# Modulation for the first norm in two column groups, x in four pieces at the head of the queue, and the sample keys one slot later

## The chip, the cores and the metric

The kernel runs on one core of one Trainium2 chip. The metric is the device time of one execution in microseconds (us), the median of several runs. TensorE (PE) multiplies, VectorE (DVE) and ScalarE (ACT) work on elements, GpSimd (POOL) and SyncE (SP) mostly issue DMAs. Each engine runs its own list of instructions in order and waits on semaphores.

## What is computed

One decoder layer, in float32, for a prompt of 512 tokens and for a sample group of 8 sequences with 4 tokens each, which attend over 4096 cached tokens.

```python
sh1, sc1, g1, sh2, sc2, g2 = split(silu(c) @ w_mod + b_mod, 6)
h = rmsnorm(x, norm1_w) * (1 + sc1) + sh1
rq, rk, rv, rg, mq, mk, mv = split(h @ w_in)
...  # retention on rq, rk, rv, rg; block-sparse attention (MoBA) on mq, mk, mv
x = x + g1 * (concat([ret_out, moba_out]) @ w_out)
h2 = rmsnorm(x, norm2_w) * (1 + sc2) + sh2
x = x + g2 * ((silu(h2 @ w_gate) * (h2 @ w_up)) @ w_down)
```

## The kernel before

**Slots.** The engines share a numbering of slots, one tile of 128 weight columns against the 512 prompt tokens in each. Slots 0 to 27 (`NT` = 28) hold the input projection, 13 to 28 also the prompt's attention, 30 to 42 retention (four pairs of heads, three slots each), 43 to 50 the output projection, 51 to 53 the second norm, 54 to 97 the gate and up tiles, 98 to 121 the down tiles. A tile is 24 matmuls of 512 columns: the high part of the weights with the high and the low part of the activations, and the low part of the weights with the high part of the activations. ScalarE makes the high halves (`split_hi`, L561; `split_out`, L566), VectorE the low ones (`split_in_place`, L1603; `split_out`, L1596).

**Keys and values of the sample group.** Beside the tiles each slot s takes group s of the gathered cache (64 groups, eight per sequence): POOL gathers K (L478), VectorE transposes it (`turn_keys`, L1634), TensorE multiplies it with the queries (`keys`, L1027), and 12 slots later (`LAG`) `weigh` (L1082) multiplies the probabilities with V. After the eighth group of a sequence the engines work through its tail, one step in each of the next slots, by t = s mod 8: at 0 the block sums (L1640) and `block_gates` (L1053), at 1 the selection (L1652), at 2 `row_max` (L1674), at 3 the bias (L1680), the exponentials on ScalarE (L590) and the first turn of the probabilities, at 4 `fold_heads` of the sequence before (L1695), at 5 the denominators, at 6 their inverse and the block diagonal of a coming sequence (L1623), at 7 `keep_out`. In every slot `slot_head` comes before the tile and `slot_rest` behind it.

**Modulation.** `w_mod` is read in 24 chunks of 256 columns, 1 MB each. Eight of them make shift and scale of the first norm before any slot: two buffers (`raw`) alternate, so each load from the third on waits for TensorE (L404 to L407). TensorE multiplies a chunk in four groups of 32 rows (`rows_by_k`, L957), VectorE adds the groups up (`keep_mod`, `fold_groups`, four instructions), TensorE turns a pair of chunks (`turn_mod`), VectorE adds the bias (`modulation`). After the eighth come the gains, then the transposed x is scaled and shifted by ScalarE (L627), column group k by column group. The other 16 chunks come in the slots of `MOD_AT`, each loaded into `rawm` when the one before is done (`mod_in`, L578).

**The head's order.** x is one DMA of 2 MB behind the first two chunks. ScalarE squares xs and the four row blocks of x, VectorE inverts, ScalarE takes the root and scales all of x (L552). TensorE transposes x after all eight chunks, and takes `keys(0)` ahead of the first tile.

**The second norm.** In slot 51 VectorE makes the inverse of the mean square, ScalarE the root after its `slot(52)` (L849 to L851), and VectorE waits for it behind its own `slot_head(52)` (L1962, L1963) before it scales x.

Of the kernel before, what the change touches and what calls it, by code (L numbers as in the profile page):

```python
# [9 lines left out]
P = 128  # L10
# [26 lines left out]
NMOD = 6 * DM // CHUNK  # L37
NMA = 2 * DM // CHUNK
# [17 lines left out]
LAG = 12  # L56
# [12 lines left out]
S_END = NG + LAG  # L69
# [7 lines left out]
def constants():  # L77
# [18 lines left out]
    put("pad0", np.zeros((P, 6)))  # L96
    put("ones", np.ones((P, P)))
# [8 lines left out]
    put("sum_pv", (p % 32)[:, None] == ht[None, :])  # L106
# [41 lines left out]
def decoder_step(nc, x_prompt, x_sample, cache_k, cache_v, state_ret, page_table, c_prompt, c_sample,  # L148
# [74 lines left out]


# [34 lines left out]
    unit = lambda n: ffa[:, n] if n < 10 else ffb[:, n - 10]  # L259
# [35 lines left out]
    s_mev, s_mtp, s_mp = sem("mod_copied+2"), sem("mod_turned+1"), sem("mod_pair_kept+1")  # L295
# [4 lines left out]
    s_xx = sem("x_turned")  # L300
    s_xst, s_hs = sem("xs_turned"), sem("asT_ready")
# [12 lines left out]
    s_srot, s_sqt, s_sqe, s_sa = sem("s_rotated"), sem("s_qk_turned"), sem("s_qkT"), sem("s_scores")  # L314
    s_sad, s_so, s_soc, s_sot = sem("s_decayed"), sem("s_out"), sem("s_out_copied"), sem("s_out_turned")
    s_ssq, s_srs, s_srn, s_srt = sem("s_squares"), sem("s_rstd"), sem("s_normed"), sem("s_norm_turned")
    s_sas, s_ssg = sem("s_ret_mixed"), sem("s_gate_silu")
# [32 lines left out]
    B_IN = NMA // 2  # L350

# [9 lines left out]
    mod_at = lambda n: slice((NMA + n) * CHUNK, (NMA + n + 1) * CHUNK)  # L361
# [22 lines left out]
    def _(sp):  # L384
# [16 lines left out]
        sp.dma_start(xP[:, :, :], x_prompt[0].rearrange("(i p) d -> p i d", p=P)).then_inc(s_x, 16)  # L401
        sp.dma_start(xs[:, :], x_sample.rearrange("b t d -> (b t) d")).then_inc(s_xs, 16)
        sp.dma_start(pt[:, :], page_table.rearrange("b n -> (b n)").partition_broadcast(P)).then_inc(s_pt, 16)
        with sp.Fori(1, NMA // 2) as i:  # L404
            for u in range(2):
                sp.wait_ge(s_md, 2 * i + u - 1)
                chunk(u, w_mod_v, bass.ds((2 * i + u) * CHUNK, CHUNK))  # L407
        for u in range(2):
            sp.wait_ge(s_md, NMA - 1 + u)
            chunk(u, w_in_v, slice(COL_OF[u], COL_OF[u] + CHUNK))  # L410
        sp.dma_start(ct[:, P + 8:], const[:, P + 8:NA]).then_inc(s_const, 16)
        sp.dma_start(rawm[:, :, :], w_mod_v[:, :, mod_at(0)]).then_inc(s_wm, 16)
# [26 lines left out]
        sp.wait_ge(s_sas, 1)  # L439
# [35 lines left out]
    def _(pool):  # L475
# [27 lines left out]
        for g in range(2, NG):  # L503
            pool.wait_ge(s_kt, g - 1)
            gather(g)
            if g == R_PAIR + 4:
# [3 lines left out]
            if g == R_OUT + 3:  # L510
# [5 lines left out]
            if g == R_OUT + 4:  # L516
# [3 lines left out]
            if g == R_OUT + 5:  # L520
                masked_k(0)
                masked_k(1)
            if g == R_SAMPLE + 5:
                pool.wait_ge(s_so, 1)
                pool.tensor_tensor(state[:, :, :, :], state[:, :, :, :],
                                   C("c_dec_s").unsqueeze(1).unsqueeze(3).broadcast_to((P, NB_SEQ, HP, HD)), ALU.mult).then_inc(s_sdc, 1)
            if R_SAMPLE + 6 <= g < R_SAMPLE + 9:
                b = 2 * (g - R_SAMPLE - 5)
# [4 lines left out]
    def _(act):  # L533
# [5 lines left out]
        act.wait_ge(s_x, 16)  # L539
        act.drain()  # L540
        for i in range(TT):
            last = act.activation(sq[:, :], xP[:, i, :], ACT.Square, accum_out=st[:, i:i + 1])
            if i < TT - 1:
                act.drain()
# [4 lines left out]
        act.drain()  # L549
# [28 lines left out]
        def mod_in(n):  # L578
            act.wait_ge(s_md, NMA + n)
            act.dma_start(rawm[:, :, :], w_mod_v[:, :, mod_at(n)]).then_inc(s_wm, 16)  # L580
# [364 lines left out]
    def _(pe):  # L945
# [1264 lines left out]
```

## Time and profile before

| | |
|---|---|
| median of 3 runs | 1119.65 us (1116.27 to 1120.73) |
| profiled execution | 1118.47 us |
| its span, first to last instruction | 1116.6 us |
| mean granted TensorE clock | 0.927 |
| TensorE matmuls busy | 979.4 us (88%) |
| VectorE busy | 656.7 us (59%) |
| ScalarE busy | 339.4 us (30%) |
| HBM read | 260.04 MB |

The profile is of one execution, 1118.47 us long, of which the span of the instructions is 1116.6. Busy times are sums over the whole span. Where a row ends in brackets, the engine was idle that long before it, and the name behind the arrow is what ended the idle time. A granted clock of 1.00 is 2.4 GHz, 0.50 is 1.2 GHz.

### The profile page before, as it was taken

To read this page: it belongs to the slowest core of one execution; us is meant where nothing else is said; L and a number is where in the kernel's file an instruction comes from. 1 tells how busy PE (TensorE), PEld (TensorE's weight loads), DVE (VectorE), ACT (ScalarE), POOL (GpSimd) and SP (SyncE) were. 2 spreads that over 40 slices of the span, in tenths; PEclk is the share of its full clock that TensorE was granted. 3 is DMA by queue.
4 is the path that set the end of the run, shared out by engine and by line. 5 is a ranking of instruction groups with operands and counts; after the bars stand their busy time and mean duration, and the time that the engine had idled before them with its cause. 6 is when DMAs were issued, how large, how long until landed. Compare 5 with 4: busy or idle time off the path is not lost.

```text
span 1116.6 us, 20916 instructions
## 1 busy us (share of the span) xinstructions
PE 979.4 (88%) x7847; PEld 684.4 (61%) x7847; DVE 656.7 (59%) x1152; ACT 339.4 (30%) x678; POOL 91.0 (8%) x90
## 2 busy tenths in 40 slices
PE   3669999999999657467987699999999999999996
PEld 1356766766776334244753476767677777777775
DVE  3555775676676487776656657543266555553344
ACT  4331233324224324224214414333234222221113
POOL 0011110000010021101400123000000000000000
PEclk8679999999999788787988689999999999999998
DMA  9846878877777768576888567977847798887662
GB/s 294 303 150 232 309 252 280 294 263 265 272 261 261 229 229 307 189 257 208 267 300 281 188 212 249 276 226 227 272 123 216 193 233 236 226 242 237 202 227 80
DMA packets 220355, 267.01 MB, mean 239 GB/s; under 512 B 12785, under 2 KB 175929, under 8 KB 212066
## 3 DMA queue, kind: packets, MB, share of 16 engines
q1 hardware_dynamic: 111586, 123.21, 35.1%
q10 hardware_dynamic: 99456, 75.38, 22.0%
q0 software_dynamic: 9216, 67.11, 16.8%
q8 instruction: 62, 1.02, 0.4%
q14 instruction: 35, 0.29, 0.1%
HBM read 260.04 MB, written 5.64 MB: 238 GB/s over the span
## 4 chain that ended last, share of the span: by engine, by line
PE 73%; DVE 13%; DMA 5%; DVEq 3%; ACT 3%; issue 2%; SPq 1%; ACTq 0%
PE banks L1001 13%; PE banks L1002 12%; PE banks L1003 12%; PE banks L961 6%; PE banks L1016 4%; PE banks L1036 4%; PE banks L1091 4%; DVE KT L1638 4%; PE banks L1017 4%; PE banks L1018 4%; DMA raw<-in_w_mod 2%; PE banks L1179 2%; DVEq L1539 2%; DMA raw<-in_w_out 1%; PE banks L1164 1%
## 5 line engine op out<-in xcount | busy, mean ns | idle before, releaser
L1001 PE MATMUL banks<-ahi,whi 128*128 128x512 f32 x416 | 170.9, 411 | 0.0
L571 ACT ACTIVATE whi<-raw 128x1024 fp32r<-128x1024 f32 (+1 forms) x76 | 78.7, 1035 | 301.3 <-PE banks L1003 157.5
L1638 DVE STREAM_TRANSPOSE KT<-K 128x2048 f32<-128x2048 f32 x64 | 147.7, 2308 | 37.0 <-PE banks L1036 29.7
L1002 PE MATMUL banks<-alo,whi 128*128 128x512 f32 x416 | 164.2, 395 | 0.0
L1003 PE MATMUL banks<-ahi,rawlo 128*128 128x512 f32 x416 | 164.0, 394 | 0.0
L1601 DVE TENSOR_TENSOR rawlo<-raw,whi 128x1024 fp32r<-128x1024 f32 (+1 forms) x76 | 91.4, 1203 | 61.9 <-ACT whi L571 59.1
L478 POOL DMA_INDIRECT K<-in_cache_k,kidx x64 | 64.7, 1011 | 581.8 <-DVE KT L1638 538.2
L1001 PEld LDWEIGHTS banks<-ahi,whi 128*128 128x128 f32 x416 | 79.6, 191 | 31.5 <-issue 13.6
L1036 PE MATMUL banks<-KT,qbd 128*32 128x128 f32 x2048 | 75.2, 291 | 25.5 <-DVE KT L1638 24.2
L1016 PE MATMUL banks<-ahi,whi 128*128 128x512 f32 x224 | 93.6, 418 | 1.2 <-DVE rawlo L1608 0.9
L1003 PEld LDWEIGHTS banks<-ahi,rawlo 128*128 128x128 f32 x416 | 79.3, 191 | 17.7
L1002 PEld LDWEIGHTS banks<-alo,whi 128*128 128x128 f32 x416 | 79.9, 192 | 15.1
L1017 PE MATMUL banks<-alo,whi 128*128 128x512 f32 x224 | 88.7, 396 | 0.0
L1018 PE MATMUL banks<-ahi,rawlo 128*128 128x512 f32 x224 | 88.6, 396 | 0.0
L1036 PEld LDWEIGHTS banks<-KT,qbd 128*32 128x32 f32 x2048 | 57.7, 116 | 42.5 <-DVE KT L1638 20.9
L1091 PE MATMUL banks<-V,pT 128*32 128x512 f32 x368 | 54.0, 650 | 3.4 <-issue 2.0
L1016 PEld LDWEIGHTS banks<-ahi,whi 128*128 128x128 f32 x224 | 42.6, 190 | 18.3 <-issue 7.6
L1608 DVE TENSOR_TENSOR rawlo<-raw,whi 128x1024 fp32r<-128x1024 f32 x28 | 34.2, 1223 | 30.4 <-ACT whi L564 14.8
L655 ACT ACTIVATE pm<-banks,st 128x128 f32<-128x128 f32 (+3 forms) x32 | 16.6, 522 | 112.4 <-DVE st L1763 112.4
L1018 PEld LDWEIGHTS banks<-ahi,rawlo 128*128 128x128 f32 x224 | 42.8, 191 | 9.7
L1017 PEld LDWEIGHTS banks<-alo,whi 128*128 128x128 f32 x224 | 42.7, 191 | 7.7
L1551 DVE TENSOR_TENSOR xtmp<-xtmp,banks 32x256 f32<-32x256 f32 x90 | 37.5, 417 | 7.0 <-issue 0.4
(304 smaller groups left out, 1447.6 us busy)
## 6 DMA issues: line engine op xcount, KB each, us to landing
V<-in_cache_v SPq DMA_DIRECT2D x184, 256.0 KB
rawm<-in_w_mod ACTq DMA_DIRECT2D x15, 1024.0 KB
zT<-in_cache_v SPq DMA_DIRECT2D x52, 256.0 KB
raw<-in_w_in ACTq DMA_DIRECT2D x12, 1024.0 KB
raw<-in_w_gate ACTq DMA_DIRECT2D x22, 512.0 KB
raw<-in_w_up ACTq DMA_DIRECT2D x22, 512.0 KB
srw<-in_w_gate SPq DMA_DIRECT2D x22, 512.0 KB, 5.4
srw<-in_w_up SPq DMA_DIRECT2D x22, 512.0 KB, 6.7
```

Source lines behind the costliest of these rows:

```text
L571: act.activation(whi[t % 2][:, 0:kd, :], raw[u][:, 0:kd, t % 2 * P:(t % 2 + 1) * P], ACT.Copy).then_inc(s_hi, 1)
L961: last = pe.matmul(out[32 * g:32 * g + 32, 0:CHUNK], lhs(k), rhs[:, k, :], start=(first and k < 4), stop=(final and k >= kd - 4))
L1001: pe.matmul(out[:, :], whi[t % 2][:, k, :], hi(k), start=(first and n == 0), stop=False)
L1002: pe.matmul(out[:, :], whi[t % 2][:, k, :], lo(k), start=False, stop=False)
L1003: last = pe.matmul(out[:, :], low[:, k, :], hi(k), start=False, stop=(final and n == kd - 1))
L1016: pe.matmul(DB[:, :], whi[m % 2][:, k, :], ahi[:, k, :], start=(k == 0), stop=False)
L1017: pe.matmul(DB[:, :], whi[m % 2][:, k, :], alo[:, k, :], start=False, stop=False)
L1018: last = pe.matmul(DB[:, :], wlow[:, k, :], ahi[:, k, :], start=False, stop=(k == KT - 1))
L1036: last = pe.matmul(LG[32 * gq:32 * gq + 32, (g % 4) * P:(g % 4 + 1) * P], qbd[g // NGRP % 2][:, j, :], KTb[:, :, j, :], start=(jj == 0), s ...
L1091: pe.matmul(VO[32 * pg:32 * pg + 32, :], pT[:, n, 32 * pg:32 * pg + 32], bufs[pg][:, :], start=(n == 0), stop=(n == NGRP - 1)).then_inc(s_ ...
L1601: tt(rawlo[u][:, 0:kd, cols], raw[u][:, 0:kd, cols], whi[t % 2][:, 0:kd, :].bitcast(F32), ALU.subtract).then_inc(s_lo, 1)
L1638: dve.transpose(KTb[:, :, :, :], Kb[g % 2][:, :]).then_inc(s_kt, 1)
```

## The change

The modulation of the first norm is read in eight loads of another cut. Load n holds two row blocks of 128 (k = 2i and 2i + 1) and 512 columns each of shift and scale; loads 0 to 3 make column groups 0 to 3 of the first norm, loads 4 to 7 groups 4 to 7. Eight places hold them (`mod_buffer`), six at a time. x comes in four DMAs ahead of them. Only two of the four row blocks of x are scaled on ScalarE, the others on VectorE. TensorE's order in the head is written out: loads, turns of x and samples alternate. Its first tile takes the products of the high weights first and the low ones behind, and no keys stand ahead of it. `KEYS` = 1 moves all that belongs to the sample's cache one slot later, `S_OUT` to `S_DOWN` with it. The sixteen chunks in the slots start with two at slot 0 (the second in a buffer of its own) and end at slot 26; VectorE copies a chunk's four groups with one instruction and TensorE adds them while it turns them (a product with `sum_pv`). The hidden units of the FFN take their buffers in another order (`UNIT_AT`), and ScalarE's waits for what lies there are renumbered with it. Semaphores of the sample's retention are merged into two. GpSimd's extra work keeps its slots, by one group less in its own loop.

```diff
-MOD_AT = [0, 1] + list(range(2, NT, 2)) + [NT - 1]
-TURN_AT = [2] + [MOD_AT[n] + 2 for n in range(3, len(MOD_AT) - 1, 2)] + [NT]
+KEYS, LAG = 1, 12
+MOD_AT = [0, 0, 1] + list(range(2, NT - 1, 2))
+TURN_AT = [s + 2 for s in MOD_AT[1::2]]
...
-S_END = NG + LAG
+S_END = KEYS + NG + LAG
...
+    early = [at(ZT + 8192 + 2048 * i, f"early{i}", [P, 2, DM]) for i in range(3)]
+    mod_buffer = early + [two_k(rawm), two_k(raw[0]), two_k(raw[1])] + early[0:2]
...
+        def early_mod(n):
+            q, i = divmod(n, 4)
+            for a in range(2):
+                cols = slice(a * DM + q * 512, a * DM + q * 512 + 512)
+                sp.dma_start(mod_buffer[n][:, :, a * 512:(a + 1) * 512], w_mod_v[:, 2 * i:2 * i + 2, cols]).then_inc(EARLY[n][0], 16)
+        for i in range(TT):
+            sp.dma_start(xP[:, i, :], x_prompt[0, i * P:(i + 1) * P, :]).then_inc(s_x, 16)
+        for n in range(2):
+            early_mod(n)
...
+        for n in range(2, 6):
+            early_mod(n)
+        for n in range(6, NMA):
+            sp.wait_ge(s_md, n - 5)
+            early_mod(n)
+        sp.wait_ge(s_md, 5)
+        chunk(0, w_in_v, slice(COL_OF[0], COL_OF[0] + CHUNK))
+        sp.wait_ge(s_md, 6)
+        chunk(1, w_in_v, slice(COL_OF[1], COL_OF[1] + CHUNK))
+        sp.dma_start(ct[:, P + 40:], const[:, P + 40:NA]).then_inc(s_const, 16)
+        sp.dma_start(rawm[:, :, :], mod_load(0)).then_inc(s_wm, 16)
+        sp.dma_start(rawm2, mod_load(1)).then_inc(s_me[0], 16)
...
-        for i in range(TT):
+        for i in range(2):
             last = act.activation(xP[:, i, :], xP[:, i, :], ACT.Copy, scale=st2[:, i:i + 1])
         last.then_inc(s_xn, 1)
-        act.wait_ge(s_mt, 1)
...
         def slot(s):
+            s -= KEYS
+            if s < 0:
+                return
...
         for k in range(KT):
+            if k == 4:
+                act.wait_ge(s_w[0], 16)
+                split_hi(0)
+            act.wait_ge(s_mt, k // 4 + 1)
             act.wait_ge(s_xt, k + 1)
...
+        for n in range(4):
+            early_mod(n)
+        turn_early(0)
...
+        pe.wait_ge(s_xn, 2)
+        turn_x_early(0)
+        turn_x_early(1)
+        early_mod(4)
+        early_mod(5)
+        turn_x_early(2)
+        turn_x_early(3)
+        early_mod(6)
+        turn_x_early(4)
+        turn_x_early(5)
+        early_mod(7)
+        turn_early(1)
+        turn_x_early(6)
+        pe.wait_ge(s_hs, 1)
+        sample_in(0)
+        turn_x_early(7)
+        sample_in(1)
...
+        for k in range(KT):
+            pe.wait_ge(s_hlo, k + 1)
+            pe.matmul(DB[:, :], whi[0][:, k, :], ahi[:, k, :], start=(k == 0), stop=False)
+            pe.matmul(DB[:, :], whi[0][:, k, :], alo[:, k, :], start=False, stop=False)
+        pe.wait_ge(s_lo, 1)
+        for k in range(KT):
+            last = pe.matmul(DB[:, :], rawlo[0][:, k, 0:P], ahi[:, k, :], start=False, stop=(k == KT - 1))
+        last.then_inc(s_ft, 1)
+        mod_chunk(0)
+        mod_chunk(1)
+        half_tile(1, 0)
+        half_tile(1, 1)
         pe.wait_ge(s_const, 16)
-        for s in range(NT):
+        slot_head(1)
+        mod_chunk(2)
+        slot_rest(1)
+        for s in range(2, NT):
...
-            dve.wait_ge(s_md, n + 1)
-            fold_groups(mst[0:32, CHUNK * (n % 2):CHUNK * (n % 2 + 1)], src, s_mev)
+            dve.wait_ge(s_md, NMA + n + 1)
+            then(cp(mst[:, CHUNK * (n % 2):CHUNK * (n % 2 + 1)], src[:, 0:CHUNK])).then_inc(s_mev, 1)
...
+        dve.wait_ge(s_rst, 1)
+        for i in range(2, TT):
+            last = ts(xP[:, i, :], xP[:, i, :], st2[:, i:i + 1], None, ALU.mult)
+        last.then_inc(s_xn, 1)
+        early_modulation(0)
+        gains(0, 4, 8, V_N1)
...
+        for k in range(4):
+            act_lo(k, k)
+        early_modulation(1)
+        gains(4, KT, 8, V_N1)
+        sample_h(1, 0, VO)
+        for k in range(4, KT):
             act_lo(k, k)
         split_in_place(0)
```

`early_mod(n)` on TensorE is eight matmuls as before (two row blocks by four column groups of 256). `early_modulation(group)` on VectorE copies the sums of a group (one copy of 128 rows by 256), waits for two transposes (`turn_early`) and adds the bias with two instructions. `turn_x_early(k)` is four transposes, as in the loop before.

## Rows read from the trace of the kernel before

**Rows 1.** Stretches (from:to, length, busy per engine, granted clock, DMA share, GB/s).
```profile
3.00:17.00 14.00, 4.94 (x41) 2.49 (x41) 3.40 (x10) 1.12 (x2) 0.00 (x0) 1.00 1.04 349
17.00:65.80 48.80, 24.16 (x184) 12.13 (x185) 27.50 (x67) 25.09 (x36) 2.02 (x2) 0.62 0.71 239
...
388.00:521.00 133.00, 81.03 (x937) 48.29 (x929) 103.65 (x192) 38.67 (x79) 16.20 (x15) 0.81 0.69 239
598.00:629.00 31.00, 14.82 (x168) 7.12 (x161) 26.80 (x32) 20.91 (x48) 4.81 (x3) 0.63 0.71 234
```
**Rows 2.** Timeline of the head (start, length, engine, line, out<-in, count).
```profile
16.75 1.06 ACT L538 ACTIVATE sq<-xs 32x1024 f32<-32x1024 f32 x1 [12.88 <-DMA xs<-in_x_sample]
...
25.50 4.25 ACT L552 ACTIVATE xP<-xP,st 128x1024 f32<-128x1024 f32 x4
...
39.00 1.94 PE L961 MATMUL banks<-raw,cT 128*32 128x256 f32 x16 [0.99 <-DMA raw<-in_w_mod]
...
44.91 1.97 PE L991 MATMUL banks<-ct,xP 128*128 128x128 f32 x8
...
46.07 0.78 ACT L627 ACTIVATE stage<-banks,mT,gain 128x512 f32<-128x512 f32 x1 [0.69 <-PE banks L991]
...
46.88 0.63 ACT L559 ACTIVATE ahi<-stage 128x512 fp32r<-128x512 f32 x1
...
49.95 1.09 PE L991 MATMUL banks<-ct,xP 128*128 128x128 f32 x8
...
65.83 1.94 PE L1036 MATMUL banks<-KT,qbd 128*32 128x128 f32 x32 [7.20 <-DVE KT L1638]
```
**Rows 3.** Chain that ended last (start, length, what), slot 1.
```profile
75.53 7.04 DMA rawm<-in_w_mod
```
**Rows 4.** Timeline of TensorE, slots 2 to 4 (keys open a slot).
```profile
89.08 0.40 PE L978 MATMUL banks<-ct,mst 32*128 32x32 f32 x4 [1.57 <-DVE mst L1551]
...
90.48 0.63 PE L1017 MATMUL banks<-alo,whi 128*128 128x512 f32 x1
...
94.85 1.06 PE L1036 MATMUL banks<-KT,qbd 128*32 128x128 f32 x32
...
102.43 1.06 PE L1036 MATMUL banks<-KT,qbd 128*32 128x128 f32 x32
```
**Rows 5.** Timeline, waits for a folded modulation chunk.
```profile
151.99 1.07 PE L961 MATMUL banks<-raw,asT 128*32 128x256 f32 x16 [1.85 <-DVE mst L1551]
...
364.13 1.40 DVE L1551 TENSOR_TENSOR mst<-mst,banks 32x256 f32<-32x256 f32 x3
...
365.68 0.40 PE L978 MATMUL banks<-ct,mst 32*128 32x32 f32 x4 [2.69 <-DVE mst L1551]
```
**Rows 6.** Timeline of VectorE, selection in slot 33, K in slot 36.
```profile
415.46 0.18 DVE L1655 COPY sm<-banks 128x16 f32<-128x16 f32 x1 [0.52 <-PE banks L1055]
...
418.62 0.16 DVE L1672 TENSOR_TENSOR sm<-sm 128x1 f32<-128x1 f32 x1
...
445.26 2.31 DVE L1638 STREAM_TRANSPOSE KT<-K 128x2048 f32<-128x2048 f32 x1 [3.23 <-PE banks L1036]
```
**Rows 7.** Timeline of TensorE, block gates in slot 48.
```profile
577.77 0.61 PE L1055 MATMUL banks<-sm,ct 128*128 128x16 f32 x2 [4.83 <-DVEq L1650]
```
**Rows 8.** Timeline of ScalarE and VectorE, second norm, slots 51 and 52.
```profile
599.55 0.51 ACT L595 ACTIVATE pe_x<-lgs,sm 128x128 f32<-128x128 f32 x1
...
603.12 0.60 ACT L588 ACTIVATE lgs<-banks 128x512 f32<-128x512 f32 x1
...
605.35 1.28 ACT L851 ACT_TABLE_LOAD   x1
606.64 0.63 ACT L851 ACTIVATE rb<-rb 128x512 f32<-128x512 f32 x1
...
608.41 1.29 DVE L1950 TENSOR_TENSOR stage<-x2T,rb 128x512 f32<-128x512 f32 x2
```
**Rows 9.** Timeline of TensorE, keys in slot 59.
```profile
683.59 1.29 PE L1036 MATMUL banks<-KT,qbd 128*32 128x128 f32 x32 [2.41 <-DVE KT L1638]
```

More of the change, by code:

```diff
@@ L1563, in modulation @@
+            f = slice(16 + 4 * pair, 20 + 4 * pair)
+            then(tt(mT[:, f, :], src[:, 0:P].rearrange("p (f s) -> p f s", f=4)[:, :, 0:NSEQ],
                     vT[:, f].unsqueeze(2).broadcast_to((P, 4, NSEQ)), ALU.add)).then_inc(s_mp, 1)
-        def gains(f0, v0):
-            dve.scalar_tensor_tensor(gain[:, :, :], mT[:, f0:f0 + KT, :], 1.0,
-                                     vT[:, v0:v0 + KT].unsqueeze(2).broadcast_to((P, KT, NSEQ)), ALU.add, ALU.mult)
-            dve.drain().then_inc(s_mt, 1)
@@ L1570, in _ @@
-        for pair in range(NMA // 2):
-            for e in range(2):
-                keep_mod(2 * pair + e, bank[6 + e])
-            modulation(pair, bank[3])
-            if pair == 0:
-                dve.wait_ge(s_sqd, 1)
-                ts(st2[:, 8:12], st[:, 0:4], 1.0 / DM, EPS, ALU.mult, ALU.add)
-                then(ts(st2[0:S, 12:13], st[0:S, 4:5], 1.0 / DM, EPS, ALU.mult, ALU.add))
-                dve.reciprocal(st2[:, 8:12], st2[:, 8:12])
-                dve.reciprocal(st2[0:S, 12:13], st2[0:S, 12:13])
-                dve.drain().then_inc(s_rin, 1)
-            if pair == 1:
-                dve.wait_ge(s_pt, 16)
-                dve.wait_ge(s_ident, 16)
-                for g in range(GRP):
-                    q = slice(32 * g, 32 * g + 32)
-                    last = ts(kidx[q, :], pt[q, :].rearrange("p (n g) -> p n g", g=GRP)[:, :, g], 32.0, C("row32")[q, :], ALU.mult, ALU.add)
-                last.then_inc(s_idx, 1)
@@ L1588, in _, with early_modulation @@
-        dve.drain()
-        gains(8, V_N1)
+        def early_modulation(group):
+            dve.wait_ge(s_md, 4 * group + 4)
+            then(cp(mst[:, CHUNK * group:CHUNK * (group + 1)], bank[group][:, 0:CHUNK])).then_inc(s_mev, 1)
+            dve.wait_ge(s_mtp, group + 1)
+            for h in range(2):
+                pick = lambda x: x.rearrange("p (a q k h) -> p a q k h", a=2, q=2, k=2)[:, :, group, :, h]
+                dst = mT[:, 0:16, :].rearrange("p (a q k h) s -> p a q k h s", a=2, q=2, k=2)[:, :, group, :, h, :]
+                last = then(tt(dst, SB[:, h * P:(h + 1) * P].rearrange("p (a k r) -> p a k r", a=2, k=2)[:, :, :, 0:NSEQ],
+                               pick(vT[:, 0:16]).unsqueeze(3).broadcast_to((P, 2, 2, NSEQ)), ALU.add))
+            last.then_inc(s_mp, 1)
@@ new lines, in gains @@
+        def gains(k0, k1, f0, v0):
+            dve.scalar_tensor_tensor(gain[:, k0:k1, :], mT[:, f0 + k0:f0 + k1, :], 1.0,
+                                     vT[:, v0 + k0:v0 + k1].unsqueeze(2).broadcast_to((P, k1 - k0, NSEQ)), ALU.add, ALU.mult)
+            dve.drain().then_inc(s_mt, 1)
+        dve.wait_ge(s_sqd, 1)
+        ts(st2[:, 8:12], st[:, 0:4], 1.0 / DM, EPS, ALU.mult, ALU.add)
+        then(ts(st2[0:S, 12:13], st[0:S, 4:5], 1.0 / DM, EPS, ALU.mult, ALU.add))
+        dve.reciprocal(st2[:, 8:12], st2[:, 8:12])
@@ new lines, in _ @@
+        dve.reciprocal(st2[0:S, 12:13], st2[0:S, 12:13])
+        dve.drain().then_inc(s_rin, 1)
+        dve.wait_ge(s_rst, 1)
[4 more added lines that the diff above has]
+        gains(0, 4, 8, V_N1)
+        dve.wait_ge(s_pt, 16)
+        dve.wait_ge(s_ident, 16)
+        for g in range(GRP):
+            q = slice(32 * g, 32 * g + 32)
+            last = ts(kidx[q, :], pt[q, :].rearrange("p (n g) -> p n g", g=GRP)[:, :, g], 32.0, C("row32")[q, :], ALU.mult, ALU.add)
@@ L1591, in act_lo @@
+        last.then_inc(s_idx, 1)
         def act_lo(k, n):
@@ L1770, in norm @@
                     bank[0][:, 0:P].rearrange("p (h d) -> p h d", h=2), st2[:, 24:26].unsqueeze(2).broadcast_to((P, 2, HD)), ALU.mult)).then_inc(s_on, 1)
-        for s in range(NT):
+        for s in range(2, NT):
             n = s - MOBA
@@ L1958, in _ @@
         dve.reciprocal(rb[:, :], rb[:, :]).then_inc(s_r1, 1)
-        gains(32, V_N2)
+        gains(0, KT, 32, V_N2)
         split_out(KT)
```

250 lines of the change are left out of this document (127 added, 123 removed).

## The prediction

> **What bounds the kernel now.** I read the stretches of the run first, then TensorE's own idle times in order, then the neighbours of each long one. TensorE is nearly saturated wherever weight tiles run, so a microsecond saved elsewhere counts only where TensorE waits. There are three such places. Up to 65.8 us no tile runs at all: in the last 48.8 us of it TensorE is busy 24.16, at a granted clock of 0.62 [rows 1]. From 388 to 521 (retention heads) it is busy 81 of 133 us while VectorE is busy 104, and from 598 to 629 (second norm) 14.8 of 31 against VectorE's 26.8 [rows 1]: there VectorE's order of work sets the time. In the head the reader is to see two chains that run one after the other, not side by side. The prompt rows are squared from 16.75 and scaled by 29.8, but transposed only at 44.9, because eight modulation chunks come first, the last at 39.00, each chunk behind its own load; and then the first tile waits for the first K transposition as well [rows 2].
>
> **Head: loads and x.** The eight chunks stay 8.4 MB and x 2.1 MB, but the buffers now hold six chunks, so the queue need not wait for TensorE. At the 349 GB/s of 3 to 17 us [rows 1] the 10.7 MB ahead of the input weights land by about 33.5. The pieces of x come first in the queue, yet ScalarE's first square waits for xs, which stays behind the same 4.3 MB as before: I cost that move at nothing, and ScalarE starts at 16.75 as now [rows 2]. The four scalings (4.25) are shared between ScalarE and VectorE, so x is ready after two of them, at 27.6 [rows 2]. VectorE's two have no row. They are bounded below by nothing and above by twice ScalarE's 1.06, and anything up to ScalarE's own two is hidden beside them. The Trainium skill (VectorE: DVE Perf Modes, Mode 2×_2P) says a one-source fp32 pass in SBUF runs at double speed; no row of this trace shows it, and the sum would not change.
>
> **Head: to the gains.** After 27.6 TensorE does in order: two column groups of x (about 1 us each at the low clock [rows 2]), chunks 4 and 5 (1.94 each), groups 2 and 3, chunk 6, groups 4 and 5, chunk 7. That is 6 + 4 x 1.94, ending near 42 at the low clock. In the run before, the clock rose from 1.2 to 2.4 GHz between 44.91 (eight transposes in 1.97) and 49.95 (in 1.09), after unbroken work [rows 2]. TensorE is now as dense from 27 on; if the clock has risen when chunk 6 comes, chunk 7 ends at 38.5. The fold, its two transposes and the gains add 2: the second gains stand at 40.5 or 44. Groups 0 to 3 were staged meanwhile.
>
> **Head: to slot 3.** Groups 4 to 7 cost ScalarE 0.78 + 0.63 each [rows 2], then VectorE takes the last low part and the low half of the weights, about 2: tile 0 can end at 52 (high clock) or 57.5. Its 24 matmuls no longer wait for K. Modulation chunks 0 and 1 follow (2.1). Their loads, the input weights, the constants and two K gathers are 6.8 MB issued from about 33, at 349 GB/s there by 52.5, just in time. Tile 1 costs 5.6 (a slot of 7.58 less keys and one small chunk [rows 4]). VectorE's samples, K transposition and copies lie beside it. Chunk 2 is asked for when chunk 1 is done and takes 7.04 [rows 3] plus 1.1, slot 2's keys wait another 2.4 for K (2.31 [rows 6]), then tile 2, one turn and chunk 3 (7.1): slot 3 begins at 71.2 or 76.4, against 94.85 [rows 4]. Slot 2 also loses its wait of 1.57 at the turn and the half-clock stretch behind it [rows 4], which is in this sum. **Head: -23.6 or -18.4; I take -21**, and -15 to -25 as bounds, since the merging of loads could fail. The skill (TensorE: Matmul & The Clock Gate, What's actually happening) says sustained activity releases the clock; by it alone the first number would hold. Rows decide for the middle, because small matmuls with waits between them ran at the low clock up to 43 [rows 2].
>
> **Modulation folds.** Each chunk was folded by one copy and three additions (0.4 + 1.40 with drains [rows 5]), now by one copy of 128 rows; TensorE sums the four groups in the turn, same count of instructions. VectorE is hidden beside TensorE almost everywhere here, so only the waits go: 1.85 at 151.99 and 2.69 at 365.68 [rows 5]. I take -1.5 and -2.0 (what is late next is the causal maximum chain of unit 15, then ScalarE's eviction). The sixteenth chunk moves from slot 27 into the head, where it is already charged: -1.0. Bounds 0 to -6 in all.
>
> **Keys one slot later.** Every K transposition, block of gates, exponentials and V product moves one slot against the rest. In saturated slots that is neutral; the last keys now land in FFN slot 64: +0.9. Where VectorE sets the time the phase counts.
> - *Retention heads*, 388 to 521. Before, the selection (13 operations, 415.46 to 418.78) ran in slot 33 while TensorE finished the heads of the pair before [rows 6]. Now it comes in slot 34, in VectorE's chain, and VectorE idles at slot 33. As a running total that is about +5. At slot 36, where VectorE had waited 3.23 [rows 6], some of it returns: +3. There the exponentials now stand before ScalarE's staging of the heads: up to +4.7. The block fold in slot 37 makes it +6; the block diagonal leaves slot 38 and comes in 39. At slots 41 and 42 the selection lies in a TensorE stretch again, which takes 2 off. **+4**, bounds -2 to +9.
> - *Slot 48*: TensorE waited 4.83 for the block sums [rows 7], which were late behind a late weight load. Now they come in slot 49: **-3**, bounds -4 to 0.
> - *Second norm.* Before, exponentials (599.55 to 603.1) ran beside VectorE's reciprocal, and the table load and square root ended at 607.3, before VectorE was free at 608.41 [rows 8]. Now VectorE's bias for them comes one slot later, behind the reciprocal, and then it waits for the root itself. ScalarE must do exponentials 3.5, logits 0.6, table 1.28, root 0.63 [rows 8] = 6.0 with nothing beside it. The fold that stood there (under 1.8) moves behind. **+6**, bounds +3 to +7.5. The skill (ScalarE: Activation LUTs, What ACT_TABLE_LOAD costs) adds a drain of 1.38 us to each 1.28 us load, by which this would be +7.4; the root here starts 1.29 after the load starts [rows 8], so the trace disagrees and I leave the drain out.
> - *Slot 58*: TensorE already waits 2.41 for VectorE at 683.59 [rows 9]. The selection (3.3 against 1 of the row maximum) now falls into it: **+2.3**, bounds 0 to 4.
>
> The renamed semaphores, the permuted hidden buffers and the earlier places in the gather loop keep each step beside the slot where its input is ready: nothing, within 1 either way.
>
> **The sum.** -21 - 1.5 - 2 - 1 + 0.9 + 4 - 3 + 6 + 2.3 = -15.3. The profiled execution took 1118.47, which gives 1103.2. The median of the runs is 1.2 above it, so the forecast for the median is 1104.5.
>
> **The rivals.** (a) *The phase shift costs nothing*: the waits in retention only move and the norm costs its lower bound 3. That is -4 and -3, 1097.5. For it: VectorE's total work there is unchanged; against it: the root's wait is serial by the program. Chance 0.17. (b) *The head keeps its low clock and the shift is exposed at its upper bounds*: -15.5 instead of -21, retention +7, slot 48 nothing: 11.5 more, 1116. It is also the case in which the change does only half of what it says. For it: the clock of 0.62 up to 65.8; against it: even cold the chain gives 18. Chance 0.19, half of it above 1114. (c) *Slower*: the exponentials stand alone before a waiting engine, as in the norm, in all four blocks of slots 36 to 60. At 6 each that is 24, with the selections' 3.3 in four slots 37 in all, against the 10 that I charge: 1131. It decides from 25 us of exposed work on (those 10 and the 15 between forecast and median). Against it: in slots 43 to 50 and from 54 TensorE is saturated and covers them. Chance 0.05. The forecast itself, 1098 to 1111, gets 0.59.
>
> **Chances and range.** About 0.5% is what a measurement of this kernel can tell from no change, so faster is below 1114.05. The forecast, (a) and half of (b) are faster: 0.59 + 0.17 + 0.09 = 0.85. Same: 0.10, the rest of (b). Slower: 0.05, (c). The range 1094 to 1116 leaves out (c), the top of (b) and the far end of (a).
>
> **What would show it.** Slot 3's keys near 74 (71 to 77). ScalarE's first square still at about 16.7. The clock at full rate before tile 0. No wait at the turn of slot 28. In the norm a wait of about 5 to 6 us between the end of the bias and VectorE's first scaling, with exponentials, table load and root in it. A head that begins slot 3 later than 80, or a retention stretch longer by over 9, would make the forecast wrong.

## The result, and the profile after

The changed kernel takes 1129.61 us (median of 11 runs, 1122.86 to 1137.4), against 1119.65 (11 runs beside it) for the kernel before: a ratio of 1.0085, 95% interval 1.0052 to 1.0118. It is slower by some 0.85%, or 10 us. The forecast was 1104.5. Of the executions reported below, two of w_out_later's ten ran in a slower state of the chip and are left out of its ratio; all others are of one state.

| | before | after |
|---|---|---|
| profiled execution | 1118.47 us | 1129.61 us |
| span | 1116.6 us | 1127.8 us |
| mean granted clock | 0.927 | 0.936 |
| TensorE matmuls busy | 979.4 us | 989.5 us |
| VectorE busy | 656.7 us | 629.0 us |
| ScalarE busy | 339.4 us | 337.2 us |

**The head did what was forecast.** First the stretches of the changed kernel, in the columns of [rows 1], then its timeline up to slot 3, for [rows 2]:

```profile
17.00:53.93 36.93, 26.04 (x245) 15.17 (x245) 18.45 (x46) 23.88 (x35) 2.02 (x2) 0.93 0.97 349
...
174.00:325.20 151.20, 146.56 (x1350) 103.43 (x1340) 89.66 (x165) 49.30 (x134) 11.24 (x12) 0.99 0.76 260
...
388.00:521.00 133.00, 82.01 (x860) 50.05 (x860) 95.73 (x182) 35.31 (x75) 14.90 (x13) 0.77 0.62 212
```
```profile
17.78 1.06 ACT L564 ACTIVATE sq<-xs 32x1024 f32<-32x1024 f32 x1 [14.05 <-DMA xs<-in_x_sample]
...
26.57 2.17 ACT L576 ACTIVATE xP<-xP,st 128x1024 f32<-128x1024 f32 x2
...
43.55 0.50 PE L1256 MATMUL banks<-ahi,whi 128*128 128x512 f32 x1
...
75.13 1.06 PE L1073 MATMUL banks<-KT,qbd 128*32 128x128 f32 x32
```

In the first of them the reader is to see the queue full from 17 us on (349 GB/s, where it was 239), the clock at 0.93, tile 0 at 43.55 (in the kernel before the keys stood ahead of it, at 65.83, and its own first matmul came at 67.69), and slot 3's keys at 75.13 in place of 94.85. The 20 us are there. At the end they are gone, and 10 more.

**Where they went.** ScalarE splits the weights of every tile once (`whi<-raw`), so the start of that split marks the progress of the work, in each kernel alike. Tile 27's, of the kernel before and of the changed one:

```profile
337.87 1.06 ACT L564 ACTIVATE whi<-raw 128x1024 fp32r<-128x1024 f32 x1
```
```profile
325.20 1.08 ACT L587 ACTIVATE whi<-raw 128x1024 fp32r<-128x1024 f32 x1
```

That is a lead of 12.7 at tile 27, where it was 19.7 at tile 5. The table gives this difference at seven tiles (below zero: ahead of the kernel before). Tiles 5 to 27 are input projection, 31 is in the output projection behind retention, 37 lies behind the second norm, 58 and 102 in the feed-forward part. A tile is split one slot or so ahead of its matmuls: tile 27 in slot 26, tile 31 in slot 44, tile 37 in slot 53. The other rows are the experiments that add the shift or end it. The medians are of all executions, the differences of the profiled one.

| kernel | median | 5 | 15 | 27 | 31 | 37 | 58 | 102 |
|---|---|---|---|---|---|---|---|---|
| changed | 1129.6 | -19.7 | -20.9 | -12.7 | -0.7 | -1.3 | 4.9 | 9.9 |
| before_late | 1152.6 | -6.2 | -5.2 | 6.6 | 22.3 | 22.4 | 28.5 | 33.0 |
| catch55 | 1122.8 | -22.2 | -23.4 | -13.5 | -2.9 | -2.8 | 1.1 | 1.1 |
| catch31 | 1112.4 | -15.9 | -17.0 | -5.1 | 4.4 | -1.8 | -2.4 | -2.4 |
| catch15_copy_last | 1100.1 | -16.3 | -17.5 | -4.9 | -9.7 | -15.6 | -16.7 | -16.7 |
| catch7 | 1107.8 | -14.9 | -4.3 | -3.8 | -1.9 | -7.9 | -9.4 | -9.4 |
| catch7_copy_last | 1100.9 | -15.3 | -7.6 | -6.9 | -9.0 | -14.9 | -16.4 | -16.4 |
| catch2 | 1097.3 | -14.1 | -13.0 | -12.4 | -14.4 | -20.6 | -21.6 | -21.6 |

**TensorE's waits in the changed kernel**, from its timeline: slot 18, slot 28, retention (three), the second norm (two).

```profile
231.64 0.70 PE L1233 MATMUL banks<-zT 64*128 64x256 f32 x4 [2.83 <-DVE zT L1876]
...
365.04 0.66 PE L1107 MATMUL banks<-ct,pe_x 128*128 128x128 f32 x4 [1.15 <-ACT pe_x L618]
...
401.63 1.09 PE L1326 MATMUL banks<-ct,xP 128*128 128x128 f32 x4 [9.18 <-ACT x2T L734]
414.36 0.61 PE L1092 MATMUL banks<-sm,ct 128*128 128x16 f32 x2 [3.15 <-DVEq L1748]
434.75 0.58 PE L1100 MATMUL banks<-ct,sm 1*128 1x1 f32 x2 [6.79 <-DVE sm L1775]
...
614.04 1.93 PE L1073 MATMUL banks<-KT,qbd 128*32 128x128 f32 x32 [12.33 <-DVE KT L1736]
625.55 1.93 PE L1073 MATMUL banks<-KT,qbd 128*32 128x128 f32 x32 [6.45 <-DVE KT L1736]
```

All of them wait for VectorE or ScalarE, at steps of the sample attention or at prompt work beside them. The 9.18 is not new: the kernel before waits 8.24 at this place. The list made the theory to test. **Phase theory:** each loss comes from the shift of keys and their followers by one slot, against work whose cost differs from slot to slot. **Rival:** another part of the change loses it (the 128-row copies, new waits, permuted hidden buffers, loads issued earlier).

### The profile page after: what moved, and what is told of

It is laid out like the page before. It is cut to its first block, busy times and chain, and to the rows that moved or that the text cites. A ratio compares the mean times of both kernels' runs of the same rounds, so it can differ in the third digit from the quotient of the medians.

```text
span 1127.8 us, 20778 instructions
## 1 busy us (share of the span) xinstructions
PE 989.5 (88%) x7867; PEld 694.9 (62%) x7867; DVE 629.0 (56%) x1077; ACT 337.2 (30%) x676; POOL 88.4 (8%) x90
## 3 DMA queue, kind: packets, MB, share of 16 engines
q10 hardware_dynamic: 98416, 74.33, 21.6%
q0 software_dynamic: 9216, 67.11, 16.4%
## 4 chain that ended last, share of the span: by engine, by line
PE 70%; DVE 12%; ACT 6%; DMA 4%; DVEq 3%; issue 3%; ACTq 1%; SPq 1%
PE banks L1040 12%; PE banks L1041 11%; PE banks L1042 11%; PE banks L993 5%; PE banks L1053 4%; PE banks L1073 4%; PE banks L1128 4%; PE banks L1055 4%; PE banks L1054 4%; DVE KT L1736 3%; DVEq L1628 2%; DMA early<-in_w_mod 2%; PE banks L1248 2%; ACT pe_x L618 1%; DMA raw<-in_w_up 1%
## 5 line engine op out<-in xcount | busy, mean ns | idle before, releaser
L1699 DVE TENSOR_TENSOR rawlo<-raw,whi 128x1024 fp32r<-128x1024 f32 (+1 forms) x76 | 93.9, 1236 | 68.0 <-ACT whi L594 65.2
L1040 PEld LDWEIGHTS banks<-ahi,whi 128*128 128x128 f32 x416 | 79.9, 192 | 33.3 <-issue 12.4
L1041 PEld LDWEIGHTS banks<-alo,whi 128*128 128x128 f32 x416 | 80.2, 193 | 15.3
L1706 DVE TENSOR_TENSOR rawlo<-raw,whi 128x1024 fp32r<-128x1024 f32 x28 | 34.3, 1224 | 37.4 <-PE banks L993 23.5
```

The costliest lines, as they stand in the source:

```text
L1040: pe.matmul(out[:, :], whi[t % 2][:, k, :], hi(k), start=(first and n == 0), stop=False)
L1041: pe.matmul(out[:, :], whi[t % 2][:, k, :], lo(k), start=False, stop=False)
L1699: tt(rawlo[u][:, 0:kd, cols], raw[u][:, 0:kd, cols], whi[t % 2][:, 0:kd, :].bitcast(F32), ALU.subtract).then_inc(s_lo, 1)
```

## The experiments

### The shift alone, undone, and undone from a slot on

**before_late** gives the kernel before the shift and nothing else.

```diff
         def slot_head(s):
+            s -= KEYS
+            if s < 0:
+                return
             if s < NG:
                 keys(s)
```

The same lines open `slot_rest` and ScalarE's `slot`; `S_END` and GpSimd's places move with them, and the hidden buffers are permuted as in the change.

> The kernel before with nothing changed but the shift: every keys step and all that follows from it one slot later (and the hidden buffers permuted as the shift needs it). Phase theory: the sum of the five stretches, 11 + 10.5 - 6 + 6.4 + 6 + 5 = 33 slower than before, about 1150 (1142 to 1153; less if a stall of the old schedule covers some of it). If the shift is harmless by itself: 1120.

Measured: 1152.59 (1149.0 to 1158.48), ratio 1.0285 (1.0211 to 1.0359). The shift alone costs 33 (32 against the 19 runs beside it).

The **catch-ups** undo it: the changed kernel runs two steps of the attention in one slot, and from there on the phase of before.

```diff
-KEYS, LAG = 1, 12
+KEYS, LAG, CATCH = 0, 12, 7
+inner = lambda s: [s - 1] if s < CATCH else [s - 1, s] if s == CATCH else [s]
```

> The changed kernel, except that slot 7 runs two steps of the attention pipeline (keys 6 and keys 7), so that from slot 8 on keys, gates, exponentials and V products stand where they stood in the kernel before. The head, the folds and the buffers stay as changed. If the one-slot shift lost the time (phase theory): the lead of 20 at slot 17 stays, 3.5 more come at slot 28, and no stretch behind loses any: about 1097 (1094 to 1101). If something else of the change lost it (the 128-row copies, the new waits, the permuted hidden buffers, loads issued earlier): near the changed kernel, above 1120.

> The same catch-up, but in slot 31, just ahead of the retention heads. Phase theory: the 11 lost in slots 17 to 26 stay lost, while the losses of the retention heads (10.5), the second norm (6.4), slots 55 to 64 (6) and FFN slots 84 to 98 (5) go, and the gain of 6 in the output projection goes too: 22 less than the changed kernel, about 1108. If slots 17 to 26 lost nothing by the phase: like the catch-up in slot 7. If the losses behind slot 31 have another cause: above 1122.

> The same catch-up in slot 55, behind the second norm. Phase theory: only the 6 of slots 55 to 64 and the 5 of FFN slots 84 to 98 come back: about 1119 (1117 to 1121). If those two have another cause (a transfer, the permuted hidden buffers): 1128 to 1130, as the changed kernel.

Measured: slot 7 1107.83 (ratio 0.9872, 0.9802 to 0.9941), slot 31 1112.4 (0.994, 0.9899 to 0.9982), slot 55 1122.77 (1.0006, 0.997 to 1.0042). The earlier the shift ends, the less is lost, and behind tile 37 no kernel that ended it before the second norm loses anything (they gain 0.6 to 1.5). In catch55 the lead stands from tile 58 on, where the changed kernel loses 5 more. The rival falls, since all its suspects are in these kernels. Slots 7 and 31 gave 11 and 4 more than expected, and slot 55 gave 1122.8 where I had 1119 (1117 to 1121): outside my bounds, though nearer to them than to the rival's 1128 to 1130. Slot 31 began with a lead of 15.9 at tile 5 and then lost 9.5 between tiles 27 and 31; its double step was not mended, so how much of that is the step's own stays open. For slot 7 the trace says why:

```profile
120.97 0.60 ACT L613 ACTIVATE lgs<-banks 128x512 f32<-128x512 f32 x1 [8.89 <-PE banks L1078]
```

ScalarE's copy of the logits waited for keys 7, ahead of the split of the next weights. The next kernel moves it to the slot's end:

```diff
+            if s == CATCH:
+                slot(s, s)
```

> As the catch-up in slot 7, with one placement mended: ScalarE's copy of the logits for the second step of slot 7 waited 8.89 us for keys 7 and stood ahead of the split of the next weights (at 121.47 in that trace, TensorE idle 7.35 at 128.26). It now stands at the end of ScalarE's slot. If that placement is why the catch-up in slot 7 gave 1107.8 and not 1097: 8 less, about 1100, and the lead over the kernel before is still 13 or more at slot 12. If transfers limit slots 7 to 12 (keys, V pages, modulation and weights together), so that a lead can't be kept there without the shift: 1105 to 1108 as now, and TensorE waits for a load there.

Measured: 1100.87 (ratio 0.9818, 0.9756 to 0.988), the median as expected. The lead is not: I had 13 or more at slot 12, and it is 9.7. It falls from 15.3 at tile 5 to 7.6 at tile 15, for the most part at slots 8 to 10, where VectorE's second K transposition (122.81) stands behind a sample fold and TensorE waits 4.83 for it at 125.26. So I moved the double step.

> As the catch-up in slot 7 with the copy last, but in slot 2, where TensorE waits 5 us anyway for the third modulation load (5.27 at 76.26 in that kernel's trace). If the double step itself costs the 6 us that the lead falls at slots 9 and 10 (VectorE's second K transposition behind the sample fold, TensorE idle 4.83 at 125.26, then half clock): that goes, about 1095 to 1097. If the transfers of keys and modulation are the limit up to slot 5 and again where the V pages begin: 1100 or more, with longer waits for loads at slots 3 to 5.

> The catch-up in slot 15, with VectorE's and ScalarE's second step at the end of the slot. The lead of 20 (15 if the load in slot 3 comes late) is kept up to slot 15, the shift's losses of slots 18 and 26 and all later ones go. Double step 6 as in slot 7: about 1100. If it hides there: 1095. If the step weighs more beside an attention unit (slots from 12 on): 1104 or more, with a wait of TensorE over 5 near slot 16.

Measured: slot 2 1097.34 (1094.77 to 1100.99; ratio 0.9823, 0.9768 to 0.9878), slot 15 1100.08 (1097.6 to 1106.5; ratio 0.985, 0.9787 to 0.9913). In slot 2 the double step takes the place of the wait for the third modulation load: TensorE waits 0.81 for that load and 2.50 for K, and the lead stays at 12 to 14 up to tile 27.

```profile
79.17 1.82 PE L1077 MATMUL banks<-KT,qbd 128*32 128x128 f32 x32 [2.50 <-DVE KT L1744]
```

In slot 15 it cost 11.5 (lead 17.5 at tile 15, 6.0 at tile 19), where I had 6 for a median of 1100. The median fits and its term does not: the kernel gained 4.8 between tiles 27 and 31, where catch2 gained 2.0. TensorE waits for V pages there, which the double step asks for earlier:

```profile
205.20 1.05 PE L1132 MATMUL banks<-V,pT 128*32 128x512 f32 x2 [2.54 <-DMA V<-in_cache_v]
206.69 3.70 PE L1132 MATMUL banks<-V,pT 128*32 128x512 f32 x5 [0.44 <-DMA V<-in_cache_v]
```

catch2 is faster than both kernels, by 22 than before. So the shift costs 33 on the kernel before (1119.6 to 1152.6) and 32 on the rest of the change (1097.3 to 1129.6). One thing keeps this from being a clean square of four cases: catch2 still has the shift in slots 0 and 1, so in it too no keys stand ahead of tile 0. The change without any shift was not run. Of catch2's 22, 14 are there at tile 5 and 6 come between tiles 31 and 37.

### Single places of the loss

**Slot 18 and slot 26.** The selection follows an odd slot there, whose sample fold makes VectorE start late.

```diff
-            slot_head(s)
+            if not late_select:
+                slot_head(s)
             if n > 0:
                 norm(n - 1)
+            if late_select:
+                slot_head(s)
```

> The changed kernel with one pair of steps exchanged on VectorE: in slots 17 to 28 where the selection (some 3.4 us) falls (18 and 26), it stands behind the scaling of the attention unit, for which TensorE waits 2.83 at 231.64 and 3.11 at 332.03 with half-clock matmuls behind. If the parity of these slots is the cause (the selection now follows an odd slot, whose sample fold makes VectorE start late): 6 to 8 less, about 1122, and the lead over the kernel before falls by 3 instead of 11 between slots 17 and 27. If VectorE is late there for another reason: TensorE's waits stay, within 2 of the changed kernel.

Measured: 1125.71 (1116.08 to 1130.24), 3.9 less than the changed kernel, with ranges that overlap. In the trace both waits of 2.83 and 3.11 are gone, and TensorE waits for ScalarE's exponentials of the unit instead:

```profile
239.86 0.33 PE L1240 MATMUL banks<-ct,pm 128*128 128x128 f32 x1 [1.54 <-ACT pm L683]
240.69 1.66 PE L1073 MATMUL banks<-KT,qbd 128*32 128x128 f32 x32
```

The keys behind it run in part at half clock (1.66 where 1.08 is usual). From the keys of slot 17 to those of slot 28 this kernel loses 8.4, the seven others that run these slots with the shift lose 10.0 to 13.5. So the exchange pays back some 2 to 5, where I had 8. It gives nothing in slot 18 (5.7 lost from slot 18 to 20, where the changed kernel loses 4.9) and something in slot 26 (2.1 against 4.5). For the rest it moved the wait. My expectation named the first waiter, not the sum of VectorE's work ahead of the unit, and the medians' 3.9 is not clear of the spread.

**The second norm.** VectorE's bias is put ahead of the reciprocal.

```diff
+        slot_head(R_NORM + 1)
         dve.wait_ge(s_ssm, KT)
```

> The changed kernel with VectorE's bias of the exponentials ahead of the reciprocal in the second norm, so that ScalarE's exponentials (3.5) run beside the reciprocal and the root follows at once. If the serial exponentials are the 6 lost there: the wait of VectorE for the root goes and the norm is 5 to 6 shorter, about 1124. If the norm is bound by ScalarE's table load and root anyway: 2 or less.

Measured: 1127.66 (1120.41 to 1135.08), 2 less. Locally it is clearer. VectorE's first scaling, in the changed kernel and in this one:

```profile
605.48 1.29 DVE L2056 TENSOR_TENSOR stage<-x2T,rb 128x512 f32<-128x512 f32 x2 [6.19 <-ACT rb L879]
```
```profile
605.13 1.29 DVE L2056 TENSOR_TENSOR stage<-x2T,rb 128x512 f32<-128x512 f32 x2 [0.55 <-ACT rb L879]
```

The wait falls from 6.19 to 0.55. From the K transposition of group 51 to that of group 56 the changed kernel takes 56.4 us (591.2 to 647.6), this one 52.5, the kernel before 50.4. The serial exponentials were 4 of the 6; the median shows half of it, within its spread.

**The sample's output weights.** In the changed kernel SyncE's loads stand just ahead of ScalarE's, which land late:

```profile
812.74 1.14 SPq L469 DMA_DIRECT2D srw<-in_w_out  x2
```
```profile
814.35 2.28 ACTq L746 DMA_DIRECT2D raw<-in_w_up  x1
...
827.10 1.06 ACT L594 ACTIVATE whi<-raw 128x1024 fp32r<-128x1024 f32 x1 [8.79 <-DMA raw<-in_w_up]
```

```diff
         sp.wait_ge(s_kt, NG)
+        sp.wait_ge(s_w[w_buffer(16)[0]], w_buffer(16)[1])
```

> The changed kernel, with SyncE's first two loads of the sample's output weights (2 MB, issued at 812.74, just ahead of ScalarE's gate and up loads at 813.95) held back until that gate and up load has landed. If the collision of these loads, which the shift made, costs what the changed kernel loses at FFN tiles 24 to 26: ScalarE's wait of 8.79 for w_up falls to about 3, 3 to 4 us less in all, 1126. If the loads are not the cause: tiles 24 to 26 lose 3.7 against the kernel before as now.

Measured: 1126.15 (1117.62 to 1136.06), 3.5 less, in a spread that does not set it apart from the changed kernel (ratios 1.0064, 1.002 to 1.0109, and 1.0085, 1.0052 to 1.0118). The trace is clearer: ScalarE waits 3.13 for TensorE in place of 8.79 for the load, and the kernel hardly moves from tile 58 (2.9 behind) to 64 (3.2 behind), where the changed kernel goes from 4.9 to 8.6. Of that loss of 3.7 the collision was 3.4.

**The order of x.**

> The changed kernel with the four pieces of x behind the first two modulation loads in the queue instead of ahead of them. ScalarE's first square waits for the sample rows, which stay behind the same bytes: within 2 of the changed kernel either way, ScalarE's first prompt square within 0.5 of 17.8. Rival: the order matters, because the first modulation chunks then start 6 us earlier and the first group of gains with them: tile 0 starts 3 or more earlier than 43.55 and the kernel is 3 or more faster.

Measured: 1128.43 (1121.54 to 1133.76), tile 0 at 43.81. The order is worth nothing at tile 0, though the first chunks start earlier and ScalarE's squares too (the sample rows' at 16.59, where the changed kernel has 17.78; the first prompt square at 17.81, where it has 19.00). My expectation had mistaken 17.8 for the first prompt square of the changed kernel. Its timeline:

```profile
11.18 3.64 PE L1183 MATMUL banks<-early,cT 128*32 128x256 f32 x32
22.51 1.93 PE L1183 MATMUL banks<-early,cT 128*32 128x256 f32 x16 [7.69 <-DMA rawm<-in_w_mod]
```

TensorE gets two chunks 6.8 us earlier, then waits 7.69 for the third and runs it at half clock (1.93 for 16 matmuls; 1.07 in the changed kernel).

**The clock in retention.** catch7_copy_last loses 4.3 of its lead between the K transpositions of groups 33 and 37 (12.6 to 8.3), with the phase and the order of before. The change: the root of the attention heads' variance goes behind `keep_x(2)` on ScalarE.

> The catch-up in slot 7 with the copy last (1100.9), and on ScalarE the root of the attention heads' variance behind the two evictions of turned x. Between 398 and 407 of that kernel's trace TensorE first waits 8.26 for such an eviction and then runs some 12 us at half clock, where the kernel before, with the same order, was back at full clock after 4; it lost 4.3 of its lead in these slots. If the clock behind the wait is the cause: without the wait the matmuls up to the keys of slot 34 run at full clock, and the lead lost there (2.8) comes back, with up to 2 beside it: 1096 to 1098. If VectorE sets the time there anyway: 1100 to 1101, as now.

Measured: 1101.15 (1100.24 to 1102.81), no gain. The wait of 8.26 went, and one of 10.16 for VectorE's block sums came in its place:

```profile
391.00 0.63 PE L1334 MATMUL banks<-ct,xP 128*128 128x128 f32 x4 [0.78 <-ACT x2T L738]
391.56 1.06 PE L1132 MATMUL banks<-V,pT 128*32 128x512 f32 x8
402.79 0.61 PE L1096 MATMUL banks<-sm,ct 128*128 128x16 f32 x2 [10.16 <-DVEq L1756]
```

VectorE sets the time there: the idle stretch moves, and the half clock behind it stays (0.61 for two matmuls that take 0.40 at full clock). What the clock alone costs was therefore not tested.

## Why the prediction was wrong, step by step

The tiles are coarse marks, since tile 27 is split in slot 26 already. Nearer to the terms of the forecast is the start of the first `keys` matmul in a slot. The differences to the kernel before at these starts (below zero: ahead; the last column is tile 102):

| kernel | 17 | 28 | 30 | 43 | 51 | 54 | 63 | end |
|---|---|---|---|---|---|---|---|---|
| before_late | -3.6 | 9.9 | 11.8 | 21.3 | 15.9 | 22.4 | 26.2 | 33.0 |
| changed | -20.1 | -9.9 | -11.4 | -1.6 | -7.8 | -1.3 | 2.7 | 9.9 |
| catch2 | -12.8 | -13.6 | -17.8 | -14.3 | -20.6 | -20.6 | -21.6 | -21.6 |
| catch15_copy_last | -5.0 | -6.1 | -8.9 | -9.7 | -15.7 | -15.7 | -16.7 | -16.7 |

What the shift costs in a stretch is what the changed kernel loses there beyond catch2. Forecast and measured, in us:

| slots | forecast | measured |
|---|---|---|
| 17 to 28, saturated | 0 | 11.0 |
| 28 to 30 | 0 | 2.7 |
| 30 to 43, retention | +4 | 6.3 |
| 43 to 51, output projection | -3 | 0.1 |
| 51 to 54, second norm | +6 | 6.5 |
| 54 to 63 | +2.3 | 5.0 |
| behind 63 | +0.9 | 7.2 |
| sum | 10.2 | 38.8 |

The step that failed is "In saturated slots that is neutral": slots that I costed at nothing took 11.0 and 2.7, and those at the end, costed at 0.9, took 7.2. Against the 38.8 stands a lead that is 7.3 larger at slot 17 than catch2's; 5.6 of it is there at tile 5 already, where executions of one and the same order of work differ by as much (see the last section). These are differences of single executions.

- **Head, -21.** Right in size: slot 3's keys at 75.13 (forecast near 74, bounds 71 to 77), a lead of 19.7 at tile 5, full clock ahead of tile 0. The Trainium skill (TensorE: Matmul & The Clock Gate, What's actually happening) says that sustained work releases the clock; here the trace agrees, with 1.07 for the 16 matmuls of a chunk from 34.16 on and 0.39 to 0.40 a matmul from tile 0's second on. Two misses offset each other, and that is luck. Tile 0 ended at 49.3, ahead of the 52 that I had for the high clock. From there to slot 3 I had 19, and it took 25.9: TensorE waited 1.41 and 2.17 for the two modulation loads that I had "just in time", and behind the second it ran at half clock from 53.93 to 59, which is some 3 us more by my estimate from the rows (1.93 for a chunk in place of 1.07, 0.63 in place of 0.40 for a matmul of the tile). Nor did I see how much of the lead is the shift's own doing: before_late leads by 6.2 at tile 5 with the old head, since no keys and no K transposition stand ahead of tile 0. Beside the shift the new head is worth 13.5 in this execution (19.7 against 6.2), and 9 to 10 in those that wait for the load of slot 3.
- **x first, nothing.** Right at tile 0 (x_late). ScalarE's first square came at 17.78, where I had 16.75; with x behind the first loads it comes at 16.59, so the order does cost that 1 us, and it is made up before tile 0.
- **Scaling shared with VectorE.** Its two took 1.42, inside the bounds of nothing and 2.12:

```profile
25.46 1.42 DVE L1678 TENSOR_SCALAR xP<-xP,st 128x1024 f32<-128x1024 f32 x2 [1.13 <-ACTq L573]
```

  That is 0.71 each, against 1.22 for a two-source pass of that size (L1706, mean 1224 ns), a ratio of 1.7. The double rate for one source that the Trainium skill states (VectorE: DVE Perf Modes, Mode 2×_2P) agrees, with a fixed part beside it by these two rows.
- **Folds and the turn of slot 28, -1.5, -2, -1.** Right in kind: the wait of 2.69 [rows 5] is gone, what is late next is 1.15 for exponentials, and between the keys of slots 28 and 29 the changed kernel gains 3.6 (catch2 4.2).
- **Saturated slots are neutral.** This step failed, and it is the largest miss: 11.0 in slots 17 to 28. The forecast gave no row for it. In the kernel before TensorE has no gap there (the columns of [rows 1]):

```profile
233.00:337.00 104.00, 104.00 (x928) 72.58 (x927) 71.42 (x138) 34.75 (x99) 8.43 (x9) 1.00 0.79 274
```

  In the changed kernel it is still busy 146.56 of 151.20 us between 174.00 and 325.20, at a clock of 0.99, and yet loses 5.0 in slot 18 and, behind this window, 4.5 in slot 26. A mean over a stretch hides two such places. Neutral holds if every slot is alike. They are not: in odd slots VectorE folds a sample chunk (1.8), and the attention units have a length that changes every slot. Before, the selection stood in slots 17 and 25, behind an even slot; shifted, it stands in 18 and 26:

```profile
225.66 0.41 DVE L1638 COPY zs<-banks 32x256 f32<-32x256 f32 x1
226.14 1.40 DVE L1640 TENSOR_TENSOR zs<-zs,banks 32x256 f32<-32x256 f32 x3
227.63 0.17 DVE L1753 COPY sm<-banks 128x16 f32<-128x16 f32 x1
...
231.29 0.29 DVE L1876 TENSOR_TENSOR zT<-banks,st 128x128 f32<-128x128 f32 x1
```

  TensorE waits 2.83 for that last operation, then runs eight matmuls of the tile at half clock (0.63 each, from 233.31 on). late_select shows that exchanging two steps pays back a part only.
- **Retention, +4 (bounds -2 to +9).** Under-sized: 6.3 against catch2, 10.6 against catch15_copy_last, 9.5 for the shift alone (before_late against the kernel before). By tiles (27 to 31) it looks like 14.0, because that stretch holds slot 26 and slots 28 and 29 as well. The kernels with the shift lose 5.7 to 10.2 in slots 30 to 43, so one execution doesn't fix the size. The changed kernel's own loss there is 9.8, over the 9 that the forecast named as a sign of being wrong. The row that I did not foresee is the 6.79 at 434.75 (slot 35): in the new phase the row maximum stands behind VectorE's rotation of the next pair. But it is not added to the rest. The kernel before waits in the same slot, behind the same rotation, for the exponentials, and that wait is gone in the changed kernel:

```profile
438.56 1.11 PE L1070 MATMUL banks<-ct,pe_x 128*128 128x128 f32 x4 [5.72 <-ACT pe_x L595]
```

  Slot by slot the changed kernel loses 5.2 in slot 33 and 5.5 in slot 37 and gains in others. Which of its steps makes how much of the 6 to 11 stays open; no run exchanges them one by one.
- **Slot 48, -3.** The wait of 4.83 [rows 7] went, but the shift is not needed for it. The changed kernel gains 5.8 in slot 48 and before_late 5.5, yet the kernels with the shift undone ahead of it gain as much: all six gain 5.9 to 6.2 between tiles 31 and 37. In before_late and the changed kernel the norm behind it takes the gain back. All of them differ from the kernel before in the order of the hidden buffers; whether that, or something of the one profiled execution, freed the weight load that was late [rows 7] is open.
- **Second norm, +6.** Right in place, size and mechanism: 6.5, and a wait of 6.19 with exponentials, load and root in it. The root starts 1.29 behind the start of the table load again, without a further drain:

```profile
603.52 1.28 ACT L879 ACT_TABLE_LOAD   x1
604.81 0.63 ACT L879 ACTIVATE rb<-rb 128x512 f32<-128x512 f32 x1
```

- **Slots 54 to 64, +2.3 + 0.9.** 5.0 measured up to slot 63. **FFN slots behind it, nothing.** 7.2 measured, of which some 3.4 are the collision of loads and the rest is open. The change delays the last V pages and the sample's weights by a slot; ScalarE asks for its loads in every second slot, so the two queues that had stood apart (801.13 and 809.03 in the timeline of the kernel before) now met. I had looked at waits on engines alone, and not at when each queue issues.
- **The rivals.** (c) had the mechanism of the wrong sign right, exposed work, and at a chance of 0.05 it comes near the time (1131). That its 37 matches the 38.8 is luck: (c) has all of it in slots 36 to 60, where the shift cost some 18 from slot 30 on, and nothing in slots 17 to 29 or behind 63, which took 21. I argued that saturated slots cover the work. In slots 43 to 51 they did (0.1), in 17 to 28 and from 54 on they did not, and this is the argument that failed.

## What to carry to other kernels

A schedule with periods of two, three and eight slots has no neutral shift: before you cost a shift at nothing, lay the costliest step of each period over the slots in which it will fall, for each engine and each issuing queue. If one part of a change is a shift of phase, test it alone, and see whether the shift can end once it has done its work: catch2 ends it in slot 2 and is 22 us faster than the kernel before. And mark the progress of two kernels slot by slot: a window with TensorE 97% busy held a loss of 5 us in one slot.

## What the hardware showed

**The clock behind a wait.** In the same order of work, behind a wait of nearly the same length, full clock came back after 4 us or was still missing after 8.6. The block gates and keys of group 33, in the kernel before (wait of 8.24, end at 411.10), in catch15_copy_last (8.63, 401.85), in catch2 (8.63, 392.99) and in catch7_copy_last (8.26, 398.45):

```profile
415.03 0.40 PE L1055 MATMUL banks<-sm,ct 128*128 128x16 f32 x2 [0.98 <-DVEq L1650]
...
417.78 1.08 PE L1036 MATMUL banks<-KT,qbd 128*32 128x128 f32 x32
```
```profile
405.78 0.40 PE L1096 MATMUL banks<-sm,ct 128*128 128x16 f32 x2 [0.98 <-DVEq L1756]
...
408.53 1.08 PE L1077 MATMUL banks<-KT,qbd 128*32 128x128 f32 x32
```
```profile
396.93 0.61 PE L1096 MATMUL banks<-sm,ct 128*128 128x16 f32 x2 [0.98 <-DVEq L1756]
...
401.64 1.93 PE L1077 MATMUL banks<-KT,qbd 128*32 128x128 f32 x32
```
```profile
402.38 0.61 PE L1096 MATMUL banks<-sm,ct 128*128 128x16 f32 x2 [0.98 <-DVEq L1756]
...
407.09 1.93 PE L1077 MATMUL banks<-KT,qbd 128*32 128x128 f32 x32
```

In the first two the clock is full 3.9 us behind the wait's end, in the others the keys 8.6 behind it still run at 1.2 GHz. So do the keys of catch7 and catch31 at this place, behind waits of 8.2. The half clock puts these keys 2.0 later behind the wait's end (8.65 in catch2, 6.68 in the kernel before). By group 37 the four kernels with it lose 4.3 to 5.3 of lead, where catch15_copy_last gains 0.5; that all of it comes from the clock is not shown. What decides it is open; it is a term of some 4 us that a row of one execution can't promise for another kernel.

**The load of slot 3.** Kernels that do the same up to slot 6 had leads of 14.9 to 16.5 (seven of them) or of 19.7 to 22.2 (three) at tile 5. In the former TensorE waits 4.7 to 5.7 for a modulation load at 75 to 77 us, in the latter not. The changed kernel's profile is one of the three, so its 19.7 at tile 5 may be the better case of its head. Whether this is also why the executions of one kernel spread (1120.41 to 1135.08 in norm_bias) is open.
